# A mixture-of-experts weight stream: asking for gate and up blocks before the down block, and giving slots back by halves

## What is computed

```python
def moe_swiglu(h, router_w, router_b, w_gu, w_down):
    logits = (h @ router_w).astype(jnp.float32) + router_b.astype(jnp.float32)
    top_v, top_i = lax.top_k(logits, TOP_K)          # 2 of 8 experts a token
    gates = jax.nn.softmax(top_v, axis=-1)
    combine = jnp.einsum('btk,btke->bte', gates, jax.nn.one_hot(top_i, N_EXPERTS, dtype=jnp.float32))
    y = jnp.zeros(h.shape, jnp.float32)
    for e in range(N_EXPERTS):                        # w_gu[e]: 1024 x 7168, w_down[e]: 3584 x 1024
        y = y + combine[..., e:e + 1] * swiglu(h, w_gu[e], w_down[e]).astype(jnp.float32)
    return y.astype(h.dtype)
```

## Time and profile before

| | us |
|---|---|
| median of 3 runs | 1429.72 (1427.49 to 1429.83) |
| profiled execution, its own time | 1431.04 |
| its span, first to last instruction | 1429.4 |
| PE busy | 1262.8 (88%) |
| DVE busy | 748.8 (52%) |
| ACT busy | 324.1 (23%) |

### The profile page before, as it was taken

How to read it: one execution, slowest core, us unless ns; L and a number is a source line. 1 busy time by engine, 2 the same in 40 slices (tenths; PEclk the granted TensorE clock), 3 DMA queues, 4 the chain that set the end, 5 groups by cost and what they waited for, 6 DMA issues and landing times.

```text
span 1429.4 us, 38408 instructions
## 1 busy us (share of the span) xinstructions
PE 1262.8 (88%) x15789; PEld 793.1 (55%) x15789; DVE 748.8 (52%) x1108; ACT 324.1 (23%) x708; POOL 41.4 (3%) x42
## 2 busy tenths in 40 slices
PE   4898998999988589978997998999799889989992
PEld 1457966888877555544553554455455445545551
DVE  0597837777753645534552544455344535534544
ACT  1006644333333321111111111111111111111111
POOL 1010000000000120000000000000000000000001
PEclk9899999999999599999998998999999989989997
DMA  9995021788897137999999999999999999999995
GB/s 340 392 344 182 26 89 58 275 294 295 296 385 284 52 116 264 395 393 393 376 396 394 377 393 394 395 379 393 393 395 395 393 393 379 396 393 393 380 395 199
DMA packets 198763, 460.18 MB, mean 322 GB/s; under 512 B 8481, under 2 KB 34129, under 8 KB 198609
## 3 DMA queue, kind: packets, MB, share of 16 engines
q1 hardware_dynamic: 184112, 403.72, 76.1%
q0 software_dynamic: 13952, 55.58, 10.5%
q10 hardware_dynamic: 672, 0.54, 0.1%
HBM read 455.74 MB, written 4.06 MB: 322 GB/s over the span
## 4 chain that ended last, share of the span: by engine, by line
issue 64%; PE 25%; DMA 5%; DVE 4%; ACT 1%; POOL 1%; SPq 0%; POOLq 0%; DVEq 0%; ACTq 0%
PE ps L800 4%; PE ps L628 3%; PE ps L756 2%; PE ps L758 2%; PE ps L757 2%; DMA ctx_tok<-in_ctx 2%; PE ps L746 2%; PE ps L688 2%; DMA ada<-in_ada_w 1%; DMA f_raw<-in_ffn_w_gu 1%; PE ps L677 1%; PE ps L593 1%; PE ps L911 1%; DVE f_lo L1425 1%; PE ps L666 1%
## 5 line engine op out<-in xcount | busy, mean ns | idle before, releaser
L936 PE MATMUL ps<-w_gu,consts_sb 128*32 128x256 f32 x8960 | 541.4, 394 | 75.5 <-DMA w_gu<-in_moe_w_gu 73.7
L936 PEld LDWEIGHTS ps<-w_gu,consts_sb 128*32 128x32 f32 x8960 | 282.7, 113 | 280.8 <-DMA w_gu<-in_moe_w_gu 86.2
L1611 DVE COPY w_dn<-w_next 128x2048 f32<-128x2048 f32 x280 | 329.8, 1220 | 0.0
L948 PE MATMUL ps<-w_dn,consts_sb 128*32 128x256 f32 x4512 | 274.8, 384 | 1.6 <-DVE w_dn L1611 1.6
L948 PEld LDWEIGHTS ps<-w_dn,consts_sb 128*32 128x32 f32 x4512 | 149.9, 112 | 104.2 <-issue 11.2
L1603 DVE TENSOR_TENSOR consts_sb<-consts_sb,ps 128x128 f32<-128x128 f32 x140 | 40.3, 288 | 301.0 <-ACT consts_sb L1199 291.7
L1199 ACT ACTIVATE consts_sb<-ps 128x128 f32<-128x128 f32 x140 | 38.8, 277 | 572.1 <-PE ps L936 572.1
L1607 DVE TENSOR_TENSOR y_all<-y_all,ps 128x256 f32 x140 | 59.0, 422 | 178.0 <-PE ps L948 178.0
L1295 DVE SCALAR_TENSOR_TENSOR ada_acc<-ada,cols,ada_acc 128x512 f32<-128x512 f32 x140 | 105.0, 750 | 4.0
L1425 DVE TENSOR_TENSOR f_lo<-f_raw,f_hi 128x2048 fp32r<-128x2048 f32 x33 | 75.4, 2292 | 53.7 <-ACT f_hi L1086 52.6
L1086 ACT ACTIVATE f_hi<-f_raw 128x2048 fp32r<-128x2048 f32 x33 | 62.9, 1916 | 70.1 <-DMA f_raw<-in_ffn_w_gu 60.0
(11 more groups left out here) (219 smaller groups left out, 931.6 us busy)
## 6 DMA issues: line engine op xcount, KB each, us to landing
w_gu<-in_moe_w_gu SPq DMA_DIRECT2D x224, 1024.0 KB, 14.8
w_next<-in_moe_w_down SPq DMA_DIRECT2D x112, 1024.0 KB, 13.2
ada<-in_ada_w POOLq DMA_DIRECT2D x23, 2048.0 KB, 9.9
f_raw<-in_ffn_w_gu SPq DMA_DIRECT2D x44, 512.0 KB, 6.6
f_raw<-in_ffn_w_down SPq DMA_DIRECT2D x11, 1024.0 KB, 4.9
wqkv<-in_attn_w_qkv SPq DMA_DIRECT2D x3, 2048.0 KB, 19.6
wo_sb<-in_attn_w_o SPq DMA_DIRECT2D x1, 4096.0 KB, 23.5
ada_fourth<-in_ada_w POOLq DMA_DIRECT2D x1, 2048.0 KB, 29.2
```

The source lines that it names most:

```text
L936: mm = pe.matmul(ps[UNIT * t:UNIT * t + UNIT, GU_BANK, 0:2 * W], x_cur[:, k, :], gate_up_columns(w_gu[x], half, kk, t), start=(k == 0), st ...
L948: mm = pe.matmul(ps[UNIT * t:UNIT * t + UNIT, Y_BANK, 0:OW], m_actT[:, q % QW, q // QW, :], w_dn[:, q, OW * t:OW * t + OW], start=(q == 0) ...
L1611: dve.tensor_copy(w_dn[:, 2 * half:2 * half + 2, :], w_next[:, y, 2 * half:2 * half + 2, :]).then_inc(s[f"d_copied{half}"], 1)
```

## The change

Three things change in SP's `after_step`, and one in `gate_up`.

- A new semaphore `gated_half` is raised by the last product of k = 3, in the middle of each `gate_up`.
- The gate-and-up block of step t+3 is now issued first: parts 0 and 1 after `gated_half` of the step's last unit, parts 2 and 3 after its `gated`.
- The down block of step t+2 is issued behind it: its first half after `d_copied0`, its second after `d_copied1`.
- The number of transfers, their sizes, the slots and the work of the other engines are the same.

```diff
         pe.sem_inc(s["f_turned"], 1)
+        pe.sem_inc(s["gated_half"], 1)
         pe.sem_inc(s["gated"], 1)
...
                     mm = pe.matmul(ps[UNIT * t:UNIT * t + UNIT, GU_BANK, 0:2 * W], x_cur[:, k, :],
                                    gate_up_columns(w_gu[x], half, kk, t), start=(k == 0), stop=(k == KC - 1))
+                if k == KC // 2 - 1:
+                    mm.then_inc(s["gated_half"], 1)
             mm.then_inc(s["gated"], 1)
...
-        def load_down(y, e, step):
+        def load_down(y, e, step, halves=range(2)):
-            for half in range(2):
+            for half in halves:
...
             next_count(sp, left, n, digit)
             sp.reg_add(gone, gone, n)
-            at = place(step)
-            sp.wait_ge(s["d_copied1"], gone)
-            load_down(y, *at)
             sp.reg_add(step, step, GU_SLOTS - DN_SLOTS)
             if gate_up:
                 at = place(step)
+                sp.wait_ge(s["gated_half"], gone)
+                load_gate_up(x, *at, (0, 1))
                 sp.wait_ge(s["gated"], gone)
-                load_gate_up(x, *at)
-            sp.reg_add(step, step, 1 - GU_SLOTS + DN_SLOTS)
+                load_gate_up(x, *at, (2, 3))
+            sp.reg_sub(step, step, GU_SLOTS - DN_SLOTS)
+            at = place(step)
+            for half in range(2):
+                sp.wait_ge(s[f"d_copied{half}"], gone)
+                load_down(y, *at, (half,))
+            sp.reg_add(step, step, 1)
```

More of the change, by code:

```diff
@@ L301, in build @@
         w_00 w_01 w_10 w_11 w_20 w_21 d_in00 d_in01 d_in10 d_in11 d_copied0 d_copied1
-        xm_hi_ready xm_lo_ready hot_ready gathered x_parts x_parts_act x_ready gated m_silu m_act_ready turned actT_ready
+        xm_hi_ready xm_lo_ready hot_ready gathered x_parts x_parts_act x_ready gated_half gated m_silu m_act_ready turned actT_ready
         down_ready y_added y_cleared places_ready y_written picked0 picked1 f_ready
```

## The result

| | before | after |
|---|---|---|
| median of 3 runs, us | 1429.72 | 1443.46 (1443.43 to 1444.35) |
| ratio, 95% interval | | 1.0097 (1.0071 to 1.0123) |
| profiled execution, own time / span, us | 1431.04 / 1429.4 | 1443.46 / 1441.8 |

The changed kernel is 13.7 us slower. The forecast was 10.3 slower. The expert stage, taken from the first `gate_up` (507.11 before, 505.79 after) to the start of the very last `down` (1400.76 and 1413.37), grew from 893.65 to 907.58 us, by 13.9. So the whole loss is in this stage.

The account below looks back on a forecast made before the run. The weight stream was taken to bound the expert stage. Earlier restart (-6.5), late down block (+16.0), dips (+8.7) and what follows PE's last wait summed to 10.3 us later with clock loss: 1440.0 us against the median, range 1429 to 1450.

Parts of the forecast that it names:

- the dips: Stream standstills behind five-unit steps: six of 2.5 us, 15.0 against 6.3 before, so 8.7 us later.
- The bound: Expert stage: the weight stream sets the time, at 394 GB/s outside the dips, 2.66 us per 1 MiB transfer.
- Part 1, the earlier ask: First long step (step 1): with `gated_half` SP issues at 545.45, not 551.95, so the stream restarts 6.5 us earlier.
- Part 2, the order: Queue in mid-stage: down block lands 16.0 us behind its gate-and-up block, waits move to `down`, dips cost 8.7 us more.
- the six steps named: Long steps 9, 17, 25, 33, 41 and 49, forecast to have dips behind them some 130 us apart.
- the 1.9 us for a dip at the full clock: Behind a long step: stream goes on at L + 17.9 with 16.0 us queued, so it stands still 1.9 us.
- waits of 3.0 and 1.8 us in step 9: PE's new wait for the down block in step 9, in two pieces: 3.0, then 1.8 after half a `down`.
- the upper bound: Clock loss after a wait in a long step: at most 1.7 us, so a dip costs 1.9 to 3.6.
- Part 3, the end: End of the expert stage: PE's last wait near 1378.2, then 30.3 us; 10.3 us later with half of 1.7 for clock.
- That the down block is not late: Rival for the down path: the block hides as before, dips go; 12.8 us less, 1416.9; chance 0.12.
- That an empty queue restarts at once: Rival for the stream's restart: no 2.3 us ahead of the data, no dips; 5.6 us less, 1424.1; chance 0.06.
- That the half release is not had: Rival for SP's ask: parts 0 and 1 go out only with `gated`, 1.74 later; 23.4 us later, 1453.1; chance 0.06.

Follow-up runs that it names:

- E2: The changed kernel with the order alone: gate-and-up block whole after `gated`, down block whole behind it after `d_copied1`; 1465.14 us, ratio 1.0247 to the kernel before.
- E7: The changed kernel with the down block queued between gate-and-up parts 0 to 2 and part 3; 1424.85 us, ratio 0.9970 to the kernel before.
- E4: The changed kernel with VectorE copying a stretch of `x_all` in place of the landed down block, same transfers and order; 1416.85 us, ratio 0.9915 to the kernel before.
- E6: The changed kernel with the down block copied to `w_dn` only in the first unit of each step; 1443.16 us, ratio 1.0093 to the kernel before.

## Why the prediction was right, point by point

The direction and the mechanism were right. One term of the sum, the dips, was too small, and that is nearly the whole miss of 3.4 us.

**The bound.** Right. 393 or 394 GB/s stand in every long window without a hole, in all kernels, and in 560 to 1370 the rate tells the holes: 391 GB/s before, 385 after and 377 in E2 lack 6, 19 and 35 us against 394.

**Part 1, the earlier ask.** 6.5 us were forecast, 6.3 measured from the first `gate_up`. At the restart the second transfer lands 4.2 us behind the first (549.3 and 553.5) in place of 2.7. In E2 to E7, too, the second or the third transfer at this place lands 1.2 to 1.4 us late. This looks like 1.5 us lost, but is mostly not: the stream runs at 394 GB/s from 549 to 672 all the same, and the kernel before loses some tenths at several landings too. Counted from the first landing after the restart to the one that PE waits for last, without the dips and the six transfers more, the changed kernel takes only 0.3 us longer. Why one transfer lands late there stays open.

**Part 2, the order.** Right in kind, as E4 shows, and the waits moved where the text said: 80.0 us in 41 places at L955 (80 to 100 in 20 to 30 were forecast; the count is higher, as each wait has two pieces). The dips stand behind the six steps named, 130.2 to 130.8 us apart. Their size was low. Six dips of 2.5, 15.0 us, were forecast, half-way between no clock loss and some. From landing to landing they measure 2.5 to 2.6 five times and 5.2 once, 18.1. So the forecast of 2.5 met five of them, but for a wrong reason, since there was no clock loss in these.

The step that failed is the 1.9 us for a dip at the full clock. Three of its terms were 0.2 to 0.3 short each. The last unit's `gate_up` starts 13.7 us after L, the landing of the down block, and not 13.5. From there the first half of `gate_up` and SP's issue take 2.2 and not 1.74 + 0.3. A gate-and-up transfer into the empty queue lands after 5.2 to 5.3 us, not 5.0, which is what a down transfer needed. The timeline of the changed kernel, the last unit of step 9 and SP's ask:

```profile
673.48 3.66 PE L941 MATMUL ps<-w_gu,consts_sb 128*32 128x256 f32 x64
...
675.70 0.37 SPq L392 DMA_DIRECT2D w_gu<-in_moe_w_gu  x1
```

The DMA view has this transfer's time to landing:

```profile
w_gu<-in_moe_w_gu SPq DMA_DIRECT2D x1, 1024.0 KB, 5.2
```

The clock loss came in one dip of six, where 2.5 had allowed for about a third of it in each. The forecast had waits of 3.0 and 1.8 us in step 9. The first was 1.08 (the timeline of step 9 above), and 0.4 to 1.5 in five of the passes, because PE had come late from the step before. Of that, the forecast took no account. The timeline of step 8 has a wait of 4.99 us, and behind it each half of `down` takes 1.93 us in place of 1.07 and a `gate_up` 4.57 in place of 3.66. These three rows are 2.6 us longer than at the full clock:

```profile
642.63 1.93 PE L955 MATMUL ps<-w_dn,consts_sb 128*32 128x256 f32 x16 [4.99 <-DVE w_dn L1618]
645.10 1.93 PE L955 MATMUL ps<-w_dn,consts_sb 128*32 128x256 f32 x16 [0.54 <-DVE w_dn L1618]
...
647.37 4.57 PE L941 MATMUL ps<-w_gu,consts_sb 128*32 128x256 f32 x64
```

In the last pass only 1.3 us went this way in the step before (step 48, halves of 1.82 and 1.60 and a `gate_up` of 3.66), so PE came earlier, waited 2.47 and 1.41 us in the long step itself, and lost its clock there, where it lies on the path to the release. The `gate_up` behind took 5.30 us (timeline, then the windows row with the granted clock of 0.66). The loss was 2.5 us in the rows below, not the 1.7 of the upper bound, so this dip of 5.2 lies above the 3.6 that was to be the most:

```profile
1310.16 1.07 PE L955 MATMUL ps<-w_dn,consts_sb 128*32 128x256 f32 x16 [2.47 <-DVE w_dn L1618]
1312.64 1.93 PE L955 MATMUL ps<-w_dn,consts_sb 128*32 128x256 f32 x16 [1.41 <-DVE w_dn L1618]
...
1314.91 5.30 PE L941 MATMUL ps<-w_gu,consts_sb 128*32 128x256 f32 x64
```

```profile
1310.00:1320.00 10.00, 8.43 (x97) 3.82 (x101) 4.13 (x6) 0.28 (x1) 0.00 (x0) 0.66 1.05 388
```

E6 has the same picture: one long step of six with a first wait of 2.5 us and a dip of 5.2, five with first waits of 0.4 to 1.5 and dips of 2.5 to 2.7.

**Part 3, the end.** Right. The last down block that PE waits for landed at about 1380.7 (forecast 1378.2), and from there to the end of the last `turn`, at 1411.7, it was 31.0 us. Forecast were 30.3 and 0.9 for the clock. With the 39.1 us of the kernel before, the order's own share at the end is 16.0 - 8.1 = 7.9.

**The sum.** In the stage: -6.3 for the restart, +7.9 for the order at the end with its clock loss, +12.0 for the dips (18.1 against 6.1), +0.3 for the late landings, which makes 13.9, as measured. The forecast had -6.5, +8.1 and +8.7. So 3.3 us of the miss are the dips.

**The rivals.** That the down block is not late is out: PE waits 80.0 us for it, and E4, which does not need it, is 26.6 us faster. The price of this rival left out the same 5.3 us as the expectation of E4. That an empty queue restarts at once is out: 5.0 to 5.3 us from issue to landing at every restart of the changed kernel in mid-stage. Behind the issue at 675.70, windows of half a us show 0 GB/s until 676.5, then 70, 94 and 238, and 389 only from 678.0. That the half release is not had is out by the issue at 675.70, within the `gate_up` that releases it. E2 is the kernel without it (and without the halves of the down ask); its price, 23.4 as forecast, is 36.4 there. Four-unit steps open holes too, 5.2 us, and the long dips are 30.8 us against 26.4.

## What to carry to other kernels

In a stream-bound stage, put into one queue first what is used first: a prefetch by one step more for one operand puts it ahead of the other, and the slots of both are then released by the later landing. Compute, for the longest step, the time from the landing that PE waits for to the next ask, add what an empty queue needs before its data are on the way (here 2.3 to 2.6 us), and compare it with what is queued behind that landing. A wait may change its name at no cost as long as the first is smaller (E7), and costs on every pass once it is larger. A stretch at the lower clock moves later waits as well as the release, so follow it through the step before too. To ask earlier, look first for a slot that is held without need (a copy repeated for each unit) rather than for an order that lets one ask pass another.

## What the runs showed of the hardware

One transfer of 1 MiB on a full queue takes 2.66 us (394 GB/s). Into an empty one, after SyncE issues it, a down transfer lands in 4.8 to 5.1 us (five dips and the restart of the kernel before) and a gate-and-up transfer in 5.0 to 5.3 (the changed kernel). At the restart in the first pass the second or third one behind it lands 3.8 to 4.2 us after the one ahead, not 2.7, in each kernel that begins there with gate-and-up parts.

In the changed kernel, E2 and E6 each wait of PE for the down copy of 2.5 us or more in the steady stretch is followed by a stretch at the lower clock, which lengthens the `down` and `gate_up` behind it by 1.3 to 3.8 us in all. Behind those waits of 1.5 us or less with which a `down` begins, none follows. Lengths between 1.6 and 2.4 us do not occur there.
